# Two mixers and one pooling stage laid anew in a fourteen-stage transformer kernel: order of units, head products, gate rows

## What is computed

```python
def token_mixer(h, w_in, conv_w, conv_b, gate_bias, mlstm_norm_gain, w_out):
    proj = h @ w_in
    aq, ak, av, mq, mk, mv, mo, mg = jnp.split(proj, cuts, axis=-1)
    aq = partial_rotary(split_heads(aq, ATT_HEADS), positions) * (ATT_HEAD_DIM ** -0.5)
    ak = partial_rotary(split_heads(ak, ATT_HEADS), positions)
    attn_out = merge_heads(dilated_attention_mixture(aq, ak, av))     # 8 heads of 64
    qk = conv(concatenate([mq, mk]), conv_w)                          # 5 taps along the tokens
    mq, mk = jnp.split(jax.nn.silu(qk + conv_b), 2, axis=-1)          # 4 heads of 128
    gates = mg.reshape(b, s, 4, 4) + gate_bias                        # 16 gate columns
    cell = mlstm(mq, mk, mv, gates 0, 1) + flipped mlstm(..., gates 2, 3)
    cell = cell * lax.rsqrt(jnp.mean(cell * cell, axis=-1) + 1e-6)
    mlstm_out = jax.nn.sigmoid(mo) * (merge_heads(cell) * mlstm_norm_gain)
    return jnp.concatenate([attn_out, mlstm_out], axis=-1) @ w_out

def _pool_mixer(xn, w_pool, scale):   # window means less x, a 256x256 product per group, times scale
```

## Time and profile before

| | |
|---|---|
| median of 3 runs | 2077.58 us |
| profiled execution | 2077.63 us, span 2075.8 us |
| PE busy | 2045.4 us, 99% of the span |
| DVE busy | 1671.8 us, 81% |
| ACT busy | 1017.0 us, 49% |
| chain that ended last | PE 91%, DVE 5%, ACT 2%, issue 1%, POOL 1% |
| granted TensorE clock | 0.999 of full speed |
| PE waits for DVE in the two mixers together | a_prob (line 1854) 3.5 us, out_lo (line 1863) 2.3 us, Y (lines 1830, 1832) 1.0 us |

### The profile page before, as it was taken

One profiled execution on the slowest core, in us unless ns is written; L12 is line 12 of the kernel. 1 busy time (PEld: TensorE's weight loads), 2 busy tenths in 40 slices (PEclk: granted clock), 3 DMA queues, 4 the chain that ended last, 5 costly groups with the idle time before them and its releaser, 6 DMA issues.

```text
span 2075.8 us, 26739 instructions
## 1 busy us (share of the span) xinstructions
PE 2045.4 (99%) x10322; PEld 1731.7 (83%) x10322; DVE 1671.8 (81%) x2798; ACT 1017.0 (49%) x1204; POOL 107.4 (5%) x237
## 2 busy tenths in 40 slices
PE   7999999999999999999999999999999999999998
PEld 7988877888978888988888889888888888988887
DVE  5788788886579886788889886989888977788986
ACT  4455445445555444454454445755445444575442
POOL 0010010000010000000010000010001000001000
PEclk9999999999999999999999999999999999999999
DMA  8476555756446656566566656346656656535662
GB/s 277 163 238 229 192 180 185 224 190 203 156 145 208 201 183 203 165 221 196 190 207 226 191 182 200 119 149 216 195 191 207 227 189 194 176 112 182 193 195 89
DMA packets 290959, 393.77 MB, mean 190 GB/s; under 512 B 9892, under 2 KB 256980, under 8 KB 290704
## 3 DMA queue, kind: packets, MB, share of 16 engines
q1 hardware_dynamic: 284032, 368.22, 54.5%
q10 hardware_dynamic: 4032, 14.68, 2.3%
q0 software_dynamic: 2768, 9.15, 1.6%
HBM read 390.95 MB, written 2.12 MB: 189 GB/s over the span
## 4 chain that ended last, share of the span: by engine, by line
PE 91%; DVE 5%; ACT 2%; issue 1%; POOL 1%; DMA 0%; SPq 0%; POOLq 0%; ACTq 0%; DVEq 0%
PE psum L552 27%; PE psum L554 27%; PE psum L553 27%; PE psum L579 2%; PE psum L582 2%; PE psum L586 2%; DVE w_lo L1510 1%; PE psum L675 1%; ACT squares L1171 1%; DVE conv_tmp L1598 0%; DVE X L1987 0%; DVE mqk L1598 0%; PE psum L1050 0%; DVE Y L1537 0%; ACT a_prob L1325 0%
## 5 line engine op out<-in xcount | busy, mean ns | idle before, releaser
L1510 DVE TENSOR_TENSOR w_lo<-raw,w_hi 128x2048 fp32r<-128x2048 f32 x349 | 794.5, 2288 | 138.6 <-ACT w_hi L1145 135.6
L1145 ACT ACTIVATE w_hi<-raw 128x2048 fp32r<-128x2048 f32 x349 | 662.8, 1908 | 117.2 <-PE psum L554 81.7
L552 PE MATMUL psum<-w_hi,xT 128*128 128x512 f32 (+1 forms) x1424 | 553.0, 388 | 1.0 <-DVE xT L1690 1.0
L554 PE MATMUL psum<-w_hi,xT 128*128 128x512 f32 (+1 forms) x1424 | 549.2, 386 | 0.0
L553 PE MATMUL psum<-w_lo,xT 128*128 128x512 f32 (+1 forms) x1424 | 549.0, 386 | 0.0
L1561 DVE STREAM_TRANSPOSE h_turned<-h_full 32x128 f32<-32x128 f32 x1408 | 426.6, 303 | 21.1
L552 PEld LDWEIGHTS psum<-w_hi,xT 128*128 128x128 f32 x1424 | 267.5, 188 | 56.2 <-DVE xT L1690 1.7
L554 PEld LDWEIGHTS psum<-w_hi,xT 128*128 128x128 f32 x1424 | 267.4, 188 | 54.1
L553 PEld LDWEIGHTS psum<-w_lo,xT 128*128 128x128 f32 x1424 | 267.5, 188 | 53.4
L552 PE MATMUL psum<-w_hi,h_hi 128*128 128x512 f32 x768 | 299.5, 390 | 0.0
L553 PE MATMUL psum<-w_lo,h_hi 128*128 128x512 f32 x768 | 298.9, 389 | 0.0
(11 more groups left out here) (226 smaller groups left out, 1663.5 us busy)
## 6 DMA issues: line engine op xcount, KB each, us to landing
raw<-in_ffn_w_in SPq DMA_DIRECT2D x176, 512.0 KB, 4.8
raw<-in_ffn_w_gate SPq DMA_DIRECT2D x88, 512.0 KB, 4.0
raw<-in_ffn_w_up SPq DMA_DIRECT2D x88, 512.0 KB, 5.0
raw<-in_ffn_w_down SPq DMA_DIRECT2D x44, 1024.0 KB, 4.9
raw<-in_ffn_w_out SPq DMA_DIRECT2D x44, 1024.0 KB, 4.9
raw<-in_conv_w_in SPq DMA_DIRECT2D x20, 1024.0 KB, 5.5
raw<-in_mix_w_in SPq DMA_DIRECT2D x16, 1024.0 KB, 5.4
raw<-in_mix_w_in SPq DMA_DIRECT2D x24, 512.0 KB, 4.7
```

The lines of the kernel that those rows point to most:

```text
L552: pe.matmul(dst, l_hi, r_hi, start=first, stop=False, skip_group_check=loose)
L554: return pe.matmul(dst, l_lo, r_hi, start=False, stop=last, skip_group_check=loose)
L1145: return act.activation(dst, source, ACT.Copy, **kw)
L1510: dve.tensor_tensor(w_lo[u % LO_RING][:], raw[u % LO_RING][:], f32(w_hi[hi_slot[u]][:]), ALU.subtract).then_inc(lo_ready, 1)
```

## The change

The units for the first two cell heads' keys and queries (`mk` 0, `mq` 0) go to places 2 and 3, ahead of those for the attention. The rest of each list follows: `LOGIT_UNITS` and `CELL_UNITS` name the units at which logits and cell sums are done. `head_out` becomes `pair_out(j)`: four matmuls, each of 64 value columns into its own 64 rows of the result, alternating between the two heads; `av_wide` becomes `av_pair` without zeros, and POOL's fill and its semaphore go. In `gate_rows` the high and low gate weights stand side by side as 32 columns, one matmul in place of two, and `gate_columns` adds the two sets of rows with the table `fold`, loaded with the mixer's constants. At the end of pooling the quarters (0,0), (0,1), (1,0) are scaled before the first X update and (1,1) right after the first rows are multiplied with the next gain.

```diff
-MIX_UNITS = [("av", 0), ("mv", 0), ("aq", 0), ("ak", 0), ("aq", 1), ("ak", 1), ("mk", 0), ("mq", 0),
+MIX_UNITS = [("av", 0), ("mv", 0), ("mk", 0), ("mq", 0), ("aq", 0), ("ak", 0), ("aq", 1), ("ak", 1),
              ("mk", 1), ("mq", 1), ("av", 1), ("mv", 1), ("mo", 0), ("mo", 1)]
+CELL_UNITS = (9, 10, 12, 13)
+LOGIT_UNITS = (7, 8, 10, 11)
-MIX_LOADS = 7
+MIX_LOADS = 8
...
                 def gate_rows(h, part):
-                    G = pair(7)[0:16, :, :]
                     rows = slice(h * P, (h + 1) * P)
-                    for k in range(part * KC // 2, (part + 1) * KC // 2):
-                        pe.matmul(G[:, :, rows], wg_hi[:, k, :], xT[:, k, :, rows], start=k == 0, stop=False,
-                                  skip_group_check=True)
-                        mm = pe.matmul(G[:, 0, rows], wg_lo[:, k, :], xT_hi[:, k, rows], start=False,
-                                       stop=k == KC - 1, skip_group_check=True)
+                    for j in range(4):
+                        k = 4 * part + j
+                        mm = pe.matmul(pair(7)[0:32, :, rows],
+                                       wg_both[:, k, :, :].rearrange("p a n -> p (a n)"), xT[:, k, :, rows],
+                                       start=k == 0, stop=k == KC - 1, skip_group_check=True)
...
+                def pair_out(j):
+                    pe.wait_ge(at_ready, b_at + 2 * j + 2)
+                    if j in (1, 2):
+                        pe.wait_ge(head_ready, b_head + j)
+                    if j == 2:
+                        pe.wait_ge(in_read, b_in + 12)
+                    elif j == 3:
+                        pe.wait_ge(in_read, b_in + 14)
                     for k in range(2):
-                        mm = pe.matmul(psum[:, 2 if hd < 6 else 5, 0:S], av_wide[:, hd // 2, k, beside],
-                                       a_probT[hd % 2][:, k, :], start=hd % 2 == 0 and k == 0,
-                                       stop=hd % 2 == 1 and k == 1, skip_group_check=True)
+                        for n in range(2):
+                            half = slice(64 * n, 64 * n + 64)
+                            mm = pe.matmul(psum[half, 2 if j < 3 else 5, 0:S], av_pair[:, j, k, half],
+                                           a_probT[n][:, k, :], start=k == 0, stop=k == 1, skip_group_check=True)
```

PE's list, ahead of and behind the second half of unit n:

```diff
-                    if n >= 10:
-                        sums(2 * (n - 10))
-                    if 7 <= n < 11:
-                        head_out(n - 7)
-                    elif n >= 12:
-                        head_out(n - 8)
+                    if n in (9, 10, 12, 13):
+                        sums(2 * CELL_UNITS.index(n))
+                    if n in (9, 10, 12):
+                        turn_weights({9: 1, 10: 3, 12: 5}[n])
+                    if n == 11:
+                        pair_out(1)
                     part_of(n, 1).then_inc(unit_used, 1)
                     if n == 3:
                         source_rows()
                     elif n == 4:
                         maxima_columns()
-                    if n >= 6:
-                        turn_weights(n - 6)
-                    if n >= 10:
-                        sums(2 * (n - 10) + 1)
-                    if 9 <= n < 13:
-                        key_query(n - 9)
-                    if n in (5, 7, 9, 11):
-                        pair_logits((n - 5) // 2)
+                    if n in (9, 12):
+                        pair_out({9: 0, 12: 2}[n])
+                    if n in (8, 9, 11, 12, 13):
+                        turn_weights({8: 0, 9: 2, 11: 4, 12: 6, 13: 7}[n])
+                    if n in (9, 10, 12, 13):
+                        sums(2 * CELL_UNITS.index(n) + 1)
+                    if n in (7, 9, 11, 12):
+                        key_query((7, 9, 11, 12).index(n))
+                    if n in LOGIT_UNITS:
+                        pair_logits(LOGIT_UNITS.index(n))
```

ACT's list, the turned heads at the top of n and the SiLU at its end:

```diff
+                    if n in (9, 10, 12):
+                        turned()
...
-                    if n in (8, 10):
+                    if n in (5, 10):
                         for k in range(2):
-                            q_or_k(n - 8 + k)
+                            q_or_k(k if n == 5 else 2 + k)
```

DVE's list:

```diff
-                    if n >= 10:
-                        head_cell(2 * (n - 10))
-                    if n == MIX_CONV_UNITS[-1] + 1:
+                    if n == 10:
                         q_or_k_conv(3)
                     if n == 3:
                         sources()
-                    if n == 3:
                         running_maxima()
                     if n == 5:
                         stabilisers()
-                        attn_weights(0)
-                        attn_weights(1)
-                    if 3 <= n < 7:
-                        rotary_position(n - 3)
-                    if 9 <= n < 13:
-                        weights(2 * (n - 9))
+                    if n in (8, 11):
+                        first = 0 if n == 8 else 4
+                        weights(first)
+                        weights(first + 1)
+                    if 5 <= n < 9:
+                        rotary_position(n - 5)
+                    if n in (9, 12):
+                        first = 0 if n == 9 else 4
+                        head_cell(first)
+                        weights(first + 2)
+                        head_cell(first + 1)
+                        weights(first + 3)
+                    if n == 10:
+                        head_cell(2)
+                        head_cell(3)
+                        low_of_heads(0)
+                    if n == 11:
+                        low_of_heads(1)
                     if n == 13:
+                        head_cell(6)
                         low_of_heads(2)
+                        head_cell(7)
...
+                    if n in LOGIT_UNITS:
+                        j = LOGIT_UNITS.index(n)
+                        attn_logits(2 * j)
+                        attn_logits(2 * j + 1)
                     if n < 13:
                         advance(u + n + 4)
                     if n == 1:
                         logs()
-                    elif n == 4:
-                        attn_logits(0)
-                        attn_logits(1)
+                    elif n == 5:
                         for d in range(2):
                             mask_exponents(d)
+                    if n in LOGIT_UNITS:
+                        attn_weights(2 * j)
+                        attn_weights(2 * j + 1)
                     if n in MIX_CONV_UNITS[:-1]:
                         q_or_k_conv(MIX_CONV_UNITS.index(n))
```

The end of pooling on DVE:

```diff
+                    if st["kind"] == "pool" and h == 0:
+                        pooled(0, 0)
+                        pooled(0, 1)
+                        link(pooled(1, 0))
...
+                    if st["kind"] == "pool" and h == 0:
+                        link(pooled(1, 1))
                     if h == 1 or st["kind"] not in ("attn", "mix"):
                         advance(end + 3)
                     if new["kind"] != "pool":
                         transposed(h)
```

More of the change, by code:

```diff
@@ L61, in shape_tables @@
     t["ident"] = np.eye(P)
+    t["fold"] = (i[:, None] % 16 == np.arange(16)[None, :])
     t["tri"] = np.stack([i[:, None] <= i[None, :], i[:, None] >= i[None, :], np.ones((P, P), bool)], 1)
@@ L310, in build @@
             cbuf = [sb(f"cbuf{i}", [P, 2, S + 4], scope=g) for i in range(2)]
-            av_wide = sb("av_wide", [P, 4, H, 192], scope=g)
-            av = [av_wide[:, :, h, :].rearrange("p j (a n) -> p j a n", a=3)[:, :, 0:3:2, :] for h in range(H)]
+            av_pair = sb("av_pair", [P, 4, H, P], scope=g)
+            av = [av_pair[:, :, h, :].rearrange("p j (a n) -> p j a n", a=2) for h in range(H)]
+            sb("below_conv_tmp", [P, 512], scope=g)
             conv_tmp = sb("conv_tmp", [P, 2, S], scope=g)
@@ L347, in build @@
             run_max = a_prob[1][0:4, :, :]
-            gate_parts = a_prob[2][0:16, :, :]
+            gate_parts = a_prob[2][0:32, :, :]
             a_probT = [sb(f"a_probT{i}", [P, 2, S], scope=g) for i in range(2)]
@@ L944, in gate_columns @@
                             mm = pe.matmul(bank(0)[:, 16 * h:16 * h + 16], gate_parts[:, part, h * P:(h + 1) * P],
-                                           ident[0:16, 0:16], start=part == 0, stop=part == 1)
+                                           fold[0:32, :], start=part == 0, stop=part == 1)
                     mm.then_inc(g_done, 1)
@@ L1344, in pair_result, with turned @@
                     e.then_inc(in_read, 1)
-                def turned(hd):
+                heads = iter(range(8))
+                def turned():
+                    hd = next(heads)
                     act.wait_ge(at_done, seen.next(at_done))
@@ L1382, in mix @@
                         act.wait_ge(g_done, seen.next(g_done))
-                        copy(gate_parts, pair(7)[0:16, :, :]).then_inc(gate_copied, 1)
+                        copy(gate_parts, pair(7)[0:32, :, :]).then_inc(gate_copied, 1)
```

(13 more changed lines are left out.)

99 lines of the change are left out of this document (37 added, 62 removed).

## The result

| | before | after |
|---|---|---|
| median | 2077.56 us | 2087.61 us (2085.38 to 2088.05) |
| ratio, 95% interval | | 1.0045 [1.0033, 1.0058] |
| profiled execution, span | 2077.63, 2075.8 | 2087.41, 2085.6 |
| granted TensorE clock, mean | 0.999 | 0.996 |

A forecast was written before the change was run, and what follows sets the result against it. PE, busy for 99% of the span, was taken to bound the kernel, with DVE within 7% of it in the mixer's big stretch. 2077.63 + 3.6 (both mixers) - 1.3 (pooling) = 2079.9 us, range 2071.0 to 2085.5.

The forecast's parts named there:

- The new order, walked through: Engine lists set side by side in a mixer: PE stalls of 2.7, 3.5, 2.8 and 0.6 us, result +1.8 us per mixer.
- In balance: stalls of 9.6 come for 3.4.: Per mixer, PE stalls of 9.6 us replace 3.4; 0.7 + 2.6 of work and about a microsecond of gaps go.
- Gate rows: Gate products of each mixer: 16 small matmuls go, 12 of them on the path, saving 0.7 us.
- Behind it PE has the same work: After `key_query(2)` in unit 11: unchanged PE work except two pair products (2.1) for four head products (3.4), -1.3 us.
- Head pairs: Head output products: a pair on column halves takes 1.06 us in place of 1.72, saving 2.6 us per mixer.
- End of pooling: Before the second rows' transposition: earlier scaling by DVE removes PE's 1.44 us wait, first rows 0.2 later; -1.3 us.
- rival C: Head output products: column halves run one after the other, 1.72 us a pair; total 2082.5 us, chance 0.18.
- D: Both mixers: about 8 places where PE and DVE wait for one another cost 0.3 us each; 2084.7 us, chance 0.13.
- B: Both mixers: DVE keeps up, the four stalls don't appear; 2060.7 us, chance 0.14 for the family below 2073.4.

The follow-up runs named there:

- the old order: The kernel before with the new end of pooling, joined gate columns and pair products, all lists otherwise as before: 2072.18 us, ratio 0.9974.
- the filled kernel: The changed kernel with unread matmuls ahead of PE's waits at `source_rows`, `sums(1)` and `sums(3)` in each mixer: 2082.79 us, ratio 1.0025.

## Why the prediction was wrong

*The new order, walked through.* Right in each place, with its sizes: 2.52 and 2.51 us at `source_rows` (2.7), 3.43 twice at `sums(1)` (3.5), 2.50 and 2.31 at `sums(3)` (2.8), 0 and 0.6 at `key_query(2)` (0.6). The runs bear out the reason given, the order within DVE's and ACT's lists: the first place and the fourth by a move of their own, the second and third only together. Two sums of the walk are off without weight: the terms named for the SiLU add up to some 1343.6 and not 1343.9, and the pooling's -1.44 + 0.2 is -1.2.

*"In balance: stalls of 9.6 come for 3.4."* This is the step that failed. It takes a stall to cost its own length, with the matmuls behind it at the pace of the trace of before, in which no stall of a mixer is longer than 1.7 us. The runs show 20 stalls of 2.2 us and more in the mixers of profiled executions (six in the changed kernel; four each with the early convolution moved and with one stall filled; two each with the SiLU late, the old order and two stalls filled). 16 of them are followed by half clock, each time for 3.41 us or twice that: all six stalls of 3.43 us, and ten of the fourteen of 2.24 to 2.93 us. A fall of 3.41 us costs between 0.8 us, where a later wait takes up part of it, and 1.7, where none does; the mean in a kernel is 1.1 to 1.7. Four of them are 4.5 of the 7.5 us between 2079.9 and 2087.41. The forecast had the stalls of 3.5 us in its own walk, and none of its rivals asked what they do to the clock.

The Trainium skill's page "TensorE: Matmul & The Clock Gate", section "Why this matters for your kernels", advises against idle gaps of PE between bursts of matmuls, because the clock then drops to half. That is what the trace shows, 0.50 behind the stalls; but the gaps of which it warns are longer than most of those here. It would have put the forecast's stalls of 3.5 us in question; the 2.5 us of the others a reader would count as harmless by it, and ten of those fourteen were not. The measurement decides.

*The rest of the walk* was 1.5 us a mixer short, as the filled kernel shows (2082.95 - 2077.63 + 1.3 = 6.6 for two mixers, 3.3 in place of 1.8), 3.0 in all. Its terms in the first mixer, compared with the filled kernel and with the pooling's 1.3 taken off the forecast's times: `source_rows` 1276.8 for 1276.4, `sums(1)` 1322.25 for 1321.7, and `key_query(2)` 2.7 us later than in the kernel before (1343.45, 1340.74) for 3.0 - 1.3 = 1.7, so 1.0 by then. About half of this is the term *Gate rows*: 0.7 was put down, 0.24 measured, because the work that it shortened stood ahead of a copy of ACT that the old, longer one had covered. The wait wasn't there to be seen in the trace of before; its cover had to be asked for. Another 0.5 is the sentence "Behind it PE has the same work": from `key_query(2)` to the cell's transposition the filled kernel takes 28.76 us where the kernel before took 29.56, so -0.8 for -1.3. Three turnings stand behind that place in the new list where two did, 0.44 more than I had counted. What is left, some 0.5 a mixer, is small gaps that I have not taken apart.

*Head pairs.* 1.06 forecast, 1.01 measured, on the chain of the changed kernel:

```profile
1342.61 1.01 PE psum L1052 x8
```

So column halves do overlap, and rival C is refuted. Two at a time for free would be 0.86, so 0.15 a pair is lost. That is in keeping with the drain at a change of mode that the prediction cites from the Trainium skill's page "TensorEngine Tiling (Array Packing)", but no run here shows where the 0.15 comes from.

*End of pooling.* -1.3 forecast; -1.6 by itself, and 1242.49 in place of 1243.81 (-1.3) at the first mixer's first transposition in the changed kernel. Right.

*The rivals.* D's 2084.7 is nearest in number, for a reason that the traces don't bear out: there is no new cost at the places where engines meet, beyond the 0.4 at `v_ext`. B, no stalls, was put at 2060.7; the changed kernel isn't this case, but with four entries moved it is nearly so (2066.1, with 1.5 us of waits left at `sums` and 0.8 at `v_ext` of the list's own). The missing rival was one that takes the forecast's own stalls and asks what a stall does to the engine that stands.

## What to carry over

Price a stall of a busy TensorE in two parts: its length, and the matmuls behind it at half clock; here the second part was 0.8 to 1.7 us for most stalls above 2.2 us and nothing for those up to 1.7. When units are laid anew in one engine's list, go through the lists of the others for each result that the first one waits for, and put it ahead of work that nobody asks for yet: four moved entries turned +0.45% into -0.56%. And when work is shortened, look at what it had covered: the next wait is often right behind it and in no trace yet.

## What the runs showed of the hardware that I had not expected

- The clock fell behind stalls of 2.24 to 3.43 us in kernels whose PE is 98 to 99% busy. Whether a stall of 2.24 to 2.93 us brings a fall is not fixed: of the two alike at `source_rows` one did. The executions of one kernel spread accordingly, 2.7 us in the changed kernel (four executions), 0.3 in the filled one (nine).
- More matmuls made the kernel faster: 60 unread ones of 512 columns took 4.8 us off.
- Fewer stalls need not mean fewer falls: with `sums(1)` filled two stalls that had had none got one each. What decides it stays open; no run here separates it from chance.
- Two 64-column halves of the array overlap to 1.01 us for eight records where full width takes 1.72, in either order of issue.
